# One 512-column pass through the high weights in place of two of 256, in 60 up-projection chunks

## What is computed

```python
# first block
a = jnp.square(jax.nn.relu(hn @ w_ff1[layer].astype(f32)))   # 256x1024 @ 1024x4096
...
# second block, per layer: 256x1024 @ 1024x5632
def swiglu(h, w_in, w_out):
    g, u = split_cols(h @ w_in, [D_FF_2, D_FF_2])
    return (jax.nn.silu(g) * u) @ w_out
```

## Time and profile before

| what | us |
|---|---|
| median of 3 runs | 1089.12 |
| lowest, highest | 1088.84, 1090.9 |
| the profiled execution, its own time | 1090.03 |
| its span (first to last instruction) | 1087.9 |
| TensorE matmuls busy | 1068.6 |
| TensorE weight loads busy | 1003.5 |
| VectorE busy | 673.3 |
| ScalarE busy | 575.6 |
| GpSimd busy | 45.1 |
| HBM read | 181.82 MB |

### The profile page before, as it was taken

How to read it: one execution, slowest core, us unless ns; L and a number is a source line. 1 busy time by engine, 2 the same in 40 slices (tenths; PEclk the granted TensorE clock), 3 DMA queues, 4 the chain that set the end, 5 groups by cost and what they waited for, 6 DMA issues and landing times.

```text
span 1087.9 us, 18334 instructions
## 1 busy us (share of the span) xinstructions
PE 1068.6 (98%) x7750; PEld 1003.5 (92%) x7750; DVE 673.3 (62%) x759; ACT 575.6 (53%) x720; POOL 45.1 (4%) x51
## 2 busy tenths in 40 slices
PE   7999999999999999999999999999999999999998
PEld 7999999899999989998999999999998899999998
DVE  5557776665555565866655545567989665555454
ACT  6557544464434455755743444376676563434454
POOL 0000000020000010000103100010000100000010
PEclk9999999999999999999999999999999999999999
DMA  7835434546565655345456555545533455555551
GB/s 256 258 117 176 134 131 141 179 151 225 162 198 190 190 164 169 114 145 166 154 196 195 191 194 172 183 160 174 175 107 122 160 172 201 170 194 192 182 168 40
DMA packets 138305, 184.05 MB, mean 169 GB/s; under 512 B 4176, under 2 KB 122064, under 8 KB 138224
## 3 DMA queue, kind: packets, MB, share of 16 engines
q1 hardware_dynamic: 137776, 182.29, 51.4%
q0 software_dynamic: 160, 0.52, 0.1%
q10 hardware_dynamic: 288, 0.07, 0.0%
HBM read 181.82 MB, written 1.05 MB: 168 GB/s over the span
## 4 chain that ended last, share of the span: by engine, by line
PE 90%; DVE 3%; ACT 3%; DMA 2%; issue 1%; SPq 0%; ACTq 0%; DVEq 0%
PE PS L358 88%; PE PS L366 2%; ACT WH L1020 1%; DVE WL L1590 1%; DMA RAW<-in_w_in_dram 1%; DMA RAW<-in_gla_w_in_dram 1%; DMA H<-in_x_dram 0%; ACT HS L1035 0%; ACT AR L1035 0%; DVE SC L2173 0%; DVE HS L1679 0%; SPq L2385 0%; DVE AR L2111 0%; DVE H L2113 0%; DVE H L1648 0%
## 5 line engine op out<-in xcount | busy, mean ns | idle before, releaser
L1590 DVE TENSOR_TENSOR WL<-RAW,WH 128x2048 fp32r<-128x2048 f32 (+1 forms) x170 | 379.4, 2234 | 227.7 <-ACT WH L1020 227.2
L1020 ACT ACTIVATE WH<-RAW 128x2048 fp32r<-128x2048 f32 (+1 forms) x175 | 325.0, 1860 | 134.4 <-PE PS L358 127.2
L358 PE MATMUL PS<-OH,WH 128*128 128x256 f32 x744 | 212.1, 285 | 1.1 <-DVE AR L1978 1.1
L358 PE MATMUL PS<-WH,XH 128*128 128x256 f32 (+1 forms) x632 | 211.7, 335 | 0.3 <-ACT WH L1020 0.2
L358 PE MATMUL PS<-OL,WH 128*128 128x256 f32 x744 | 210.4, 283 | 0.0
L358 PE MATMUL PS<-OH,WL 128*128 128x256 f32 x744 | 210.4, 283 | 0.0
L358 PE MATMUL PS<-WL,XH 128*128 128x256 f32 (+1 forms) x632 | 208.8, 330 | 0.0
L358 PE MATMUL PS<-WH,XL 128*128 128x256 f32 (+1 forms) x632 | 208.5, 330 | 0.0
L358 PE MATMUL PS<-XH,WH 128*128 128x256 f32 x608 | 173.8, 286 | 1.5 <-DVE WL L1590 0.8
L358 PE MATMUL PS<-XL,WH 128*128 128x256 f32 x608 | 172.0, 283 | 0.0
L358 PE MATMUL PS<-XH,WL 128*128 128x256 f32 x608 | 172.0, 283 | 0.0
(11 more groups left out here) (201 smaller groups left out, 1144.6 us busy)
## 6 DMA issues: line engine op xcount, KB each, us to landing
RAW<-in_ffn_w_in_dram SPq DMA_DIRECT2D x44, 1024.0 KB, 5.1
RAW<-in_w_ff_dram SPq DMA_DIRECT2D x32, 1024.0 KB, 5.4
RAW<-in_ffn_w_out_dram SPq DMA_DIRECT2D x22, 1024.0 KB, 4.9
RAW<-in_w_in_dram SPq DMA_DIRECT2D x20, 1024.0 KB, 5.1
RAW<-in_gla_w_in_dram SPq DMA_DIRECT2D x12, 1024.0 KB, 5.5
RAW<-in_diff_w_in_dram SPq DMA_DIRECT2D x12, 1024.0 KB, 5.2
RAW<-in_ple_w_gate_dram SPq DMA_DIRECT2D x8, 1024.0 KB, 5.1
RAW<-in_w_out_dram SPq DMA_DIRECT2D x4, 1024.0 KB, 4.9
```

Of the source, the lines that this page charges most:

```text
L358: return e.matmul(o, l, r, start=start, stop=stop, skip_group_check=skip)
L1020: act(high, raw, ACT.Copy).then_inc(s["w_hi"], 1)
L1590: e.tensor_tensor(low, raw, high.bitcast(F32), ALU.subtract).then_inc(s["w_lo"], 1)
```

## The change

The new `feat_wide` takes the place of `feat` in the feed-forward and both SwiGLU stages (16 + 22 + 22 chunks); all other products keep `feat`. It uses TWO banks per chunk, one per feature block. The high and low parts of an activation now lie in one buffer, 2048 elements apart, and one matmul of 512 columns moves both (2 ranges of 256) through the high weights: columns 0 to 255 of the bank get high x high, columns 256 to 511 low x high. A second matmul of 256 columns moves the high part through the low weights and adds into columns 0 to 255. ScalarE copies columns 256 to 511 to the arena (semaphores ff_b and sw_b), VectorE adds them to columns 0 to 255 (ff_ev, sw_g, sw_u), and the rest works from the arena. In the feed-forward VectorE does max and square in one operation (ff_sq) and ScalarE's Square is gone. Gate uses banks 0 and 1, up banks 2 and 3. The factor's matmul of round 0 moves ahead of up 0 and to bank 7, and the wait for RB ahead of the per-layer projection. ScalarE's copy of the weights behind up stands ahead of Silu in every round.

The buffers and the new functions:

```diff
-        self.XH = sb("XH", [128, 2048], F32R)
...
+        self.X, self.O = (sb(n, [128, 2, 2048], F32R) for n in "XO")
+        self.XH, self.XL, self.OH, self.OL = (x[:, i, :] for x in (self.X, self.O) for i in range(2))
...
+    def both(self, n, k):
+        return (self.X if n == "X" else self.O)[:, :, 256 * k:256 * k + 256]
...
+    def feat_wide(c, bank, ops, norm=None):
+        w, high = m.weights(c), m.pair(ops)[0]
+        ready(c)
+        for k in range(8):
+            if norm:
+                ahead(norm, k)
+            for fb in range(2):
+                wh, wl = (x[:, k, fb * 128:fb * 128 + 128] for x in w)
+                if k:
+                    mm(PS[:, bank + fb, 0:256], wl, high[:, k, :], False, False, True)
+                i = mm(PS[:, bank + fb, :], wh, m.both(ops, k), k == 0, k == 7)
+                if k == 0:
+                    mm(PS[:, bank + fb, 0:256], wl, high[:, k, :], False, False, True)
+        i.then_inc(s["gemm"], 1)
```

TensorE's program, feed-forward stage:

```diff
-            if i >= 4:
-                e.wait_ge(s["ff_ev"], i - 3)
-            feat(ff_at(i), i % 4, m.pair("O"), "g2" if i == 0 else None)
+            if i >= 2:
+                e.wait_ge(s["ff_ev"], i - 1)
+            feat_wide(ff_at(i), 2 * (i % 2), "O", "g2" if i == 0 else None)
```

TensorE's program, SwiGLU stages:

```diff
-                if i >= 2:
-                    e.wait_ge(s["sw_w"], f0 + i - 1)
-                feat(up_at(layer, i, 0), (2 * i) % 4, ops, f"nf{layer}" if i == 0 else None)
+                if i >= 1:
+                    e.wait_ge(s["sw_g"], f0 + i)
+                feat_wide(up_at(layer, i, 0), 0, ops, f"nf{layer}" if i == 0 else None)
                 if i == 0:
                     e.wait_ge(s["res"], r0)
-                feat(up_at(layer, i, 1), (2 * i + 1) % 4, ops)
+                    spread_r(f"nf{layer}", 7)
+                else:
+                    e.wait_ge(s["sw_u"], f0 + i)
+                feat_wide(up_at(layer, i, 1), 2, ops)
             if i == 0:
-                spread_r(f"nf{layer}", 3)
+                e.wait_ge(s["rb"], layer + 2)
...
-                e.wait_ge(s["rb"], layer + 2)
```

ScalarE's program, feed-forward stage:

```diff
-            e.wait_ge(s["ff_ev"], i + 1)
-            act(w, w, ACT.Square).then_inc(s["ff_sq"], 1)
+            e.wait_ge(s["gemm"], ff_at(i) + 1)
+            if i >= 2:
+                e.wait_ge(s["ff_ev"], i - 1)
+            act(v3(m.ar(1024 + 512 * (i % 2), 512), 2), PS[:, 2 * (i % 2):2 * (i % 2) + 2, 256:512], ACT.Copy).then_inc(s["ff_b"], 1)
```

ScalarE's program, SwiGLU stages:

```diff
+        def low_part(i, x):
+            n = f0 + i
+            e.wait_ge(s["gemm"], up_at(layer, i, x) + 1)
+            if i >= 2:
+                e.wait_ge(s["sw_t" if x == 0 else "sw_w"], n - 1)
+            act(v3(m.ar(5632 + 1024 * x + 512 * (i % 2), 512), 2), PS[:, 2 * x:2 * x + 2, 256:512], ACT.Copy).then_inc(s["sw_b"], 1)
...
                 hi(up_at(layer, i, 0) + 2)
+                w = m.ar(512 * (i % 2), 512)
+                low_part(i, 0)
                 if i == 0:
-                    hi(up_at(layer, 0, 1) + 2)
-                    spread_copy(1 + layer, 3)
-                w = m.ar(512 * (i % 2), 512)
+                    spread_copy(1 + layer, 7)
+                hi(up_at(layer, i, 1) + 2)
                 e.wait_ge(s["sw_t"], f0 + i + 1)
                 act(w, w, ACT.Silu).then_inc(s["sw_s"], 1)
-                if i:
-                    hi(up_at(layer, i, 1) + 2)
+                low_part(i, 1)
```

VectorE's program, feed-forward stage:

```diff
-            e.wait_ge(s["gemm"], c + 1)
...
-            e.tensor_scalar(w, u, 0.0, None, ALU.max).then_inc(s["ff_ev"], 1)
+            e.wait_ge(s["ff_b"], i + 1)
+            e.tensor_tensor(v3(w, 2), PS[:, b:b + 2, 0:256], v3(m.ar(1024 + 512 * (i % 2), 512), 2), ALU.add).then_inc(s["ff_ev"], 1)
+            e.wait_ge(s["ff_ev"], i + 1)
+            e.scalar_tensor_tensor(out=w, in0=w, scalar=0.0, in1=w, op0=ALU.max, op1=ALU.mult).then_inc(s["ff_sq"], 1)
```

VectorE's program, SwiGLU stages:

```diff
                 lo(up_at(layer, i, 0) + 2)
+                e.wait_ge(s["sw_b"], 2 * n + 1)
+                if i >= 2:
+                    e.wait_ge(s["sw_lo"], n - 1)
+                e.tensor_tensor(v3(w, 2), PS[:, 0:2, 0:256], v3(vg, 2), ALU.add).then_inc(s["sw_g"], 1)
                 if i == 0:
                     lo(up_at(layer, 0, 1) + 2)
                     e.wait_ge(s["rb"], layer + 2)
-                e.wait_ge(s["gemm"], up_at(layer, i, 0) + 1)
-                if i >= 2:
-                    e.wait_ge(s["sw_lo"], f0 + i - 1)
-                e.tensor_tensor(v3(w, 2), v3(PS[:, (2 * i) % 4, :], 2), rb, ALU.mult).then_inc(s["sw_t"], 1)
+                e.wait_ge(s["sw_g"], n + 1)
+                e.tensor_tensor(v3(w, 2), v3(w, 2), rb, ALU.mult).then_inc(s["sw_t"], 1)
                 if i:
                     lo(up_at(layer, i, 1) + 2)
-                e.wait_ge(s["sw_s"], f0 + i + 1)
-                e.wait_ge(s["gemm"], up_at(layer, i, 1) + 1)
-                e.tensor_tensor(w, w, PS[:, (2 * i + 1) % 4, :], ALU.mult).then_inc(s["sw_w"], 1)
+                e.wait_ge(s["sw_b"], 2 * n + 2)
+                e.tensor_tensor(v3(vu, 2), PS[:, 2:4, 0:256], v3(vu, 2), ALU.add).then_inc(s["sw_u"], 1)
+                e.wait_ge(s["sw_s"], n + 1)
+                e.wait_ge(s["sw_u"], n + 1)
+                e.tensor_tensor(w, w, vu, ALU.mult).then_inc(s["sw_w"], 1)
```

More of the change, by code:

```diff
@@ L183 @@
 hg_sig hg_lf hg_kq hg_one hg_ln hg_d hg_acc hg_ed hg_ex hg_p hg_s hg_acc2 hg_o
-gates mg mg_hi mg_lo ff_ev ff_sq ff_hi ff_lo n1_r pn_r nm1_r bgh fin_m fin_r fin_h
+gates mg mg_hi mg_lo ff_b ff_ev ff_sq ff_hi ff_lo n1_r pn_r nm1_r bgh fin_m fin_r fin_h
 gz gl_qk gl_l gl_m gl_abs gl_one gl_scan gl_c gl_e gl_z gl_s gl_u gl_ua gl_w gl_x gl_o gl_r8 gla_ev
-sw_t sw_s sw_w sw_hi sw_lo p_hi p_lo ple_pw ple_g ple_gg ple_h
+sw_b sw_g sw_u sw_t sw_s sw_w sw_hi sw_lo p_hi p_lo ple_pw ple_g ple_gg ple_h
 df_ev df_sq df_r df_kn df_tr df_qk df_sc df_mx df_e df_a df_ta df_at df_o df_l df_lx df_tab df_dsq df_ap df_dt df_thi df_tlo""".split()
@@ L215, in __init__ @@
         self.WL = sb("WL", [128, NW, SLOT], F32R)
-        self.XH = sb("XH", [128, 2048], F32R)
-        self.XL = sb("XL", [128, 2048], F32R)
-        self.OH = sb("OH", [128, 2048], F32R)
-        self.OL = sb("OL", [128, 2048], F32R)
+        self.X, self.O = (sb(n, [128, 2, 2048], F32R) for n in "XO")
+        self.XH, self.XL, self.OH, self.OL = (x[:, i, :] for x in (self.X, self.O) for i in range(2))
         self.H = sb("H", [128, 2048])
@@ L799, in swiglu @@
     def swiglu(layer):
-        f0, ops, ring = 11 * layer, m.pair("OX"[layer]), "XO"[layer]
+        f0, ops, ring = 11 * layer, "OX"[layer], "XO"[layer]
         r0 = 12 if layer == 0 else 20
@@ L1934, in vector_program @@
             lo(c + 2)
-            w, u = m.ar(512 * (i % 2), 512), PS[:, i % 4, :]
-            e.wait_ge(s["gemm"], c + 1)
+            w, b = m.ar(512 * (i % 2), 512), 2 * (i % 2)
             if i >= 2:
                 e.wait_ge(s["ff_lo"], i - 1)
-            e.tensor_scalar(w, u, 0.0, None, ALU.max).then_inc(s["ff_ev"], 1)
+            e.wait_ge(s["ff_b"], i + 1)
+            e.tensor_tensor(v3(w, 2), PS[:, b:b + 2, 0:256], v3(m.ar(1024 + 512 * (i % 2), 512), 2), ALU.add).then_inc(s["ff_ev"], 1)
+            e.wait_ge(s["ff_ev"], i + 1)
+            e.scalar_tensor_tensor(out=w, in0=w, scalar=0.0, in1=w, op0=ALU.max, op1=ALU.mult).then_inc(s["ff_sq"], 1)
             high, low = ring_lo(0, i)
@@ L2076, in swiglu @@
             if i < 11:
-                w = m.ar(512 * (i % 2), 512)
+                n = f0 + i
+                w, vg, vu = (m.ar(x + 512 * (i % 2), 512) for x in (0, 5632, 6656))
                 lo(up_at(layer, i, 0) + 2)
+                e.wait_ge(s["sw_b"], 2 * n + 1)
+                if i >= 2:
+                    e.wait_ge(s["sw_lo"], n - 1)
+                e.tensor_tensor(v3(w, 2), PS[:, 0:2, 0:256], v3(vg, 2), ALU.add).then_inc(s["sw_g"], 1)
                 if i == 0:
```

## The result

| kernel | median us | lowest, highest | runs |
|---|---|---|---|
| before, same series | 1090.01 | 1088.84, 1091.71 | 4 |
| the change | 1080.33 | 1079.80, 1084.01 | 4 |

The ratio is 0.9916, with a 95% interval of 0.9899 to 0.9933: faster by 9.7 us, where 1078.0 us and 11.1 us were forecast. The profiled execution took 1080.15 us (span 1078.0).

A forecast was written before the change was run, and what follows sets the result against it. TensorE's matmul stream was taken as the bound. Removing 960 matmuls gains 12.0 us, less 0.9 us of row factor waits: 11.1 us, so 1078.9 us profiled and 1078.0 us as median; range 1074.5 to 1083.2 us.

The forecast's parts named there:

- The bound and the mechanism: Three projection stages: the matmul stream sets the time, and about 13 ns of each matmul do not depend on columns.
- Matmuls: 60 feed-forward and SwiGLU chunks: three 256-column passes become one of 512 and one of 256, gaining 12.0 us.
- Copies and adds: Feed-forward and SwiGLU chunks: added ScalarE copies and VectorE adds stay covered by 6 us and more; cost nothing.
- Banks: Feed-forward and SwiGLU chunks: two chunks fill the four banks that four shared, with time enough to free them; cost nothing.
- The chain to the down projection: Last round of each stage: longer steps from last up-type chunk to down projection still finish in time; cost nothing.
- The row factor's matmul: Ahead of up 0 in both layers: TensorE waits for the diagonal, 0.45 us twice, 0.9 us lost.
- First iteration: SwiGLU's first round: the weights of up 1 are ready with 0.8 us left; cost nothing, but close.
- Rival 1: Three stages: every wide pass costs 0.232 us and up 1 comes 0.6 us late per layer; 1083.2 us, chance 0.17.
- Rivals 2 and 3: Feature chunks: wide pass slowed by its second operand range, 1102 us, chance 0.06; or wide pass split in two, 1090.0 us, 0.07.

The follow-up runs named there:

- three: The changed kernel with each 512-column pass split again into two of 256, copies, adds, banks and waits kept; 1091.09 us, ratio 1.0012 to before.
- blocks: The changed kernel with each chunk issuing its 16 wide passes first, then its 16 narrow ones; 1079.47 us, ratio 0.9900 to before.
- spread: The changed kernel with the row factor's matmul issued behind row block 1 of up 0 instead of ahead of up 0; 1081.57 us, ratio 0.9924 to before.
- contig: The changed kernel with wide passes moving 512 contiguous columns, low part's product left out, except in each stage's first chunk; 1082.48 us, ratio 0.9926 to before.

## Why the prediction was right, and where it was not

**The bound and the mechanism: right.** Matmuls stood back to back before and after, and "three" gives the gain back when nothing but the count is restored. The fixed part is 120 - 106.7 = 13.3 ns at 256 columns and 226.7 - 213.3 = 13.3 at 512. The Trainium skill's 2.5 ns ("TensorE: Matmul & The Clock Gate", Back-to-back issue gap) does not hold for this stream, in which each matmul has its own weight load; blocks shows the difference most plainly, since 960 x 2.5 ns would be 2.4 us and 12.0 were gained. The same section says, which the prediction passes over, that its formula is for a gap without a weight load, and that in a stream of load and matmul pairs the spacing at 512 columns is about 131 ns; the 226.7 ns of this trace agree with neither.

**"Matmuls": the term that was mis-sized.** The term was 12.0 us, 60 chunks with 0.20 each. Measured by the periods it is 16 x (11.22 - 11.12) + 22 x (16.98 - 16.65) = 1.6 + 7.3 = 8.9 us. I took 0.3475 us a pair as the sum of two averages, each from a stream of one width, and took "the mean over a stage, which holds both". It does not: no row of before alternates the widths, and the alternation has a price of its own, 6.7 ns a pair in the chunks with the long pattern. The lower bound of this term (0.352 a pair, 8.0 us) is near what holds there, 0.353. The order "blocks", which is made of two unmixed runs, has periods of 11.01 and 16.57: 16 x 0.21 + 22 x 0.41 = 12.4 us, a little above the term, as 13.3 ns are above the 12.5 of the forecast.

**Copies and adds: right.** Copy 597 ns (604 forecast), the add 690, the max-multiply 692, where I had taken 750 (the view of groups; columns: total us, mean ns, idle ahead of them):

```profile
L2117 DVE TENSOR_TENSOR AR<-PS,AR 128x512 f32<-128x512 f32 x11 | 7.6, 690 | 17.0 <-ACT AR L1410 17.0
```

```profile
L1410 ACT ACTIVATE AR<-PS 128x512 f32<-128x512 f32 x22 | 13.1, 597 | 58.1 <-PE PS L360 58.1
```

```profile
553.90:570.55 16.65, 16.65 (x89) 14.27 (x88) 10.33 (x9) 7.88 (x7) 0.00 (x0) 1.00 0.57 190
```

VectorE is busy 10.33 us in an iteration (10.6 forecast), ScalarE 7.88 (8.0). ScalarE waits for TensorE in 58.1 us of the stage, VectorE for ScalarE in 17.0: they follow the stream and do not lead it. **Banks: right**, no wait is listed for one.

**The chain to the down projection: right at the end, missed at the beginning.** In the last feed-forward round the residual is not delayed: the wait of the transposes behind it is 1.8 us before and after. But the chain stands in the *first* round too, where only chunk 1 covers it: add, max-multiply, copy, subtract, done at 235.04 when the stream would go on at 234.50. There it starts when VectorE's weight subtraction ends, before and after, so the new copy is hidden and the chain is no longer than before (2.80 against 2.74 us); but the matmuls that cover it became fewer. That is 0.36 us of extra wait that stood nowhere in my sum. I checked the last round, since its cover is one projection, and did not ask what covers the first.

**The row factor's matmul: right**, 0.40 and 0.37 us, 0.45 twice forecast. "spread" gives back 0.41 and 0.46. **First iteration:** the low part of up 1's weights is done at 541.55 (started at 539.26, for 2.29) and up 1 starts at 542.89, so 1.3 us were left and 0.8 forecast. Rival 1's late up 1 does not occur.

**The sum.** By measured terms: 8.9 - 0.8 - 0.4 = 7.7 us, against 7.6 in the stages and 7.8 between the runs at equal clock. It lies between forecast (11.1) and rival 1 (5.9), and nearer to rival 1, whose first half, dearer wide passes, happened in the chunks with the long pattern, and whose second, a late up 1, did not. The median, 1080.33, is in the range and 2.3 us above the forecast. The forecast was subtracted from a median, 1089.12, that stands 1.2 us above the 1087.9 of a full clock. From a full clock it would have been 1076.8, and the change took 1080.15 there, 3.3 us more. I read the clock as full in every slice of the page, but its digit 9 is 90% or more and hides the stretch at 0.50. **Rivals 2 and 3** fell by contig (nothing for the second range) and by the periods.

## What to carry to other kernels

When a kernel like this one is bound by the matmul stream and each matmul has its own weight load, 13 ns of every matmul do not depend on its columns; merging two passes that share weights gains that, 960 times here. Where wide and narrow passes must be mixed, issue them in runs of one width and not in alternation, and time the mixed order itself before you forecast from unmixed streams. A chain behind the stream must be checked in the first round as well as in the last, and even where the change leaves it as long as it was, since a shorter stream covers less of it. Gains that use up the same slack do not add. For differences under 0.5%, compare executions at an equal mean granted clock.

## What the runs showed of the hardware

- Steady spacing of float32 matmuls with a 128x128 weight load each: 120 ns at 256 columns, 226.7 at 512. Alternating the two costs 346.7 or 353.3 ns a pair by what came ahead; each chunk shows the same in every iteration.
- A moving operand of two ranges of 256 columns, 2048 elements apart, takes the same time as one range (contig).
- The granted clock can fall to its half level for a moment with TensorE busy all the time (0.50 from 439 to 442 us in before, 0.91 over 18 us). From run to run the times go with the mean clock: 1087.63 to 1092.90 for before, with mean clocks of 0.999 to 0.994.

**Open:** why the alternating order costs 6.7 ns a pair. The runs exclude the second range (contig) and show that the order decides; the trace shows the pattern with ScalarE and VectorE idle and with DMA on and off. Alternating banks alone do not cause it: in blocks every pass goes to the other bank than the one before, at 0.227 and 0.120 us. A stream with other widths was not tried. Open too is whether the 13 ns belong to the matmul or to its weight load, since every run adds or removes both together.
